# Two encoder layers with experts: low parts of split weights in place, two expert loads in the dense layer, the last unit in two loads

## The chip, the cores and the metric

The kernel runs on one core of a Trainium2 chip. A core has five engines that run side by side and meet only in semaphores: TensorE (PE), which multiplies matrices; VectorE (DVE); ScalarE (ACT); GpSimd (POOL); and SyncE (SP), which here only issues DMAs. Data come from HBM over 16 DMA engines into SBUF, 128 partitions wide; products gather in PSUM. The metric is the device time of one execution in microseconds. Before the change it is 1310.86 us, the median of three runs (1309.59 to 1312.39).

## The reference

Two layers over 256 tokens of width 1024, all float32. Each layer has a token mixer and a channel mixer, each between two norms. The channel mixer is a dense SwiGLU of width 4096 in layer 0; in layer 1 it is eight experts of width 3584, of which each token uses two.

```
for layer in range(2):
    proj = rmsnorm(h, mix_norm_pre[layer]) @ w_in[layer]            # 1024 -> 2048: u, q, k, v
    y_pool = pool_mixer(u, pool_w[layer], pool_scale[layer])         # windows of 2, 4, 8, 16 tokens
    y_na = neighbourhood_attention(q, k, v, na_rpb[layer])           # 16 heads of 32
    h = h + rmsnorm(concat(y_pool, y_na) @ w_out[layer], mix_norm_post[layer])
    hn = rmsnorm(h, ffn_norm_pre[layer])
    f = swiglu(hn, dense...) if layer == 0 else moe_swiglu(hn, router, gate, up, down)
    h = h + rmsnorm(f, ffn_norm_post[layer])
```

## The kernel before

**Split weights.** Outside the experts, PE works on float32 weights that are split in two: `w_hi`, a rounded copy that ACT makes (L1189), and `w_lo`, the rest, that DVE makes by subtraction (L1424, and L1435 for a piece of one). A product is three matmuls (L730 to L732: hi by hi, lo by hi, hi by lo). Weights arrive in 36 loads of 2 MB: 6 for the mixer of layer 0, 24 for the dense layer (gate, up, down in turns, eight blocks), 6 for the mixer of layer 1. They go round a ring of `RING` = 3 buffers (`ring`). Each load is worked in two halves, so there are 72 halves; `w_hi` and `w_lo` have `STAGE` = 3 buffers of half a load each. Three semaphores count halves: `hi_ready` (ACT's copy made), `split_ready` (DVE's rest made), `half_done` (PE's products made). Below, "half 40" is the first half of load 20.

**Who waits for what.** SP issues load n once `split_ready` says that both halves of load n-3 are split (L458), because then nobody reads the ring buffer any more. ACT copies half k when its load has landed and `half_done` has passed half k-3 (its `w_hi` buffer is free). DVE follows ACT, PE follows DVE.

**Experts.** Each expert's weights (gate, up, down) are 24 units of 3584 columns, 1.835 MB each, 192 in all, loaded by SP (L502) into 12 slots of SBUF (`SLOTS`), one after the other round the slots; unit n takes the slot of unit n-12 once PE has counted that one in `unit_done`. Most of the slots lie over memory that the mixer of layer 1 uses before them: bias table, `qT`, `kT`, `vv`, ring, `w_hi`, `w_lo`, `h`. So the first 12 units each wait for the last use of what lies below them. Slot 10 (`H_SLOT`) lies over `h` and `gpost`, which come back by two DMAs (L534, L535) once that slot is free for good; that is why `SLOT_OF` sends the last but one unit to slot 11.

**An expert on PE.** The tokens of an expert are gathered into 3 groups of 32 (in some of the eight turns, 2 groups; the order of turns is 3, 2, 3, 3, 2, 3, 3, 2). Gate and up take eight units each (L1077), down takes the last eight (L1086), two at a time: the first of a pair is used for three tiles of 1024 columns, then a fourth tile lies over both, then three tiles lie in the second. ACT applies silu (L1376), DVE multiplies and transposes (L1744, L1749), and ACT copies the result `y` out (L1382). Then PE spreads it back over the tokens (`combine`; for the last turn `combine_end`, L1047), DVE and ACT make the last norm, and SP stores the result. If an expert had more tokens than its turn holds, up to five extra turns would follow in a loop; with these inputs the loop runs through without work.

**ACT's tables.** ACT must load a table before it uses another family of functions. `last_norm` begins with such a load (L1265, for the square root), after the loop of extra turns.

## Time and profile before

| | |
|---|---|
| median of three runs | 1310.86 us (1309.59 to 1312.39) |
| span of the profiled execution | 1308.4 us |
| the profiled execution's own time | not given apart from its span; the three runs lie 1.2 to 4.0 us above the span, their median 2.5 us |
| PE busy | 1285.0 us, 98% |
| DVE, ACT, POOL busy | 409.0, 286.0, 108.4 us |
| weights and other data read from HBM | 439.36 MB |
| DMA queue of SP | 433.58 MB, 81.4% of the 16 engines' span |

The span runs from the first to the last instruction of the profiled execution; all positions below are microseconds from its start. The mixer of layer 0 fills about 10 to 98 us, the dense layer 110 to 375, the mixer of layer 1 382 to 470, norm and routing up to 489, the eight experts 489 to 1295, the last norm and the store the rest. A busy PE is not a PE at its peak: its matmuls are pipelined and their ends modelled. What counts is what it waits for.

### The profile page before, as it was taken

To read this page: it belongs to the slowest core of one execution; us is meant where nothing else is said; L and a number is where in the kernel's file an instruction comes from. 1 tells how busy PE (TensorE), PEld (TensorE's weight loads), DVE (VectorE), ACT (ScalarE), POOL (GpSimd) and SP (SyncE) were. 2 spreads that over 40 slices of the span, in tenths; PEclk is the share of its full clock that TensorE was granted. 3 is DMA by queue.
4 is the path that set the end of the run, shared out by engine and by line. 5 is a ranking of instruction groups with operands and counts; after the bars stand their busy time and mean duration, and the time that the engine had idled before them with its cause. 6 is when DMAs were issued, how large, how long until landed. Compare 5 with 4: busy or idle time off the path is not lost.

```text
span 1308.4 us, 31062 instructions
## 1 busy us (share of the span) xinstructions
PE 1285.0 (98%) x14397; PEld 794.5 (61%) x14397; DVE 409.0 (31%) x565; ACT 286.0 (22%) x433; POOL 108.4 (8%) x240
## 2 busy tenths in 40 slices
PE   9999999999999999999999999999999999999996
PEld 8888999999989863354353364345353355336443
DVE  6886555555567850030210120030030031021011
ACT  4666344444466630000000000000000000000101
POOL 3334200000000307300000000000000000000000
PEclk9999999999999989999999999999999999999999
DMA  9646855555543399999999999999999999999994
GB/s 303 221 175 211 259 193 193 193 193 193 193 158 141 146 425 427 425 421 398 427 424 426 426 424 425 425 425 425 425 424 425 425 426 424 425 426 424 426 425 187
DMA packets 67012, 443.50 MB, mean 339 GB/s; under 512 B 4520, under 2 KB 10800, under 8 KB 42304
## 3 DMA queue, kind: packets, MB, share of 16 engines
q1 hardware_dynamic: 64736, 433.58, 81.4%
q0 software_dynamic: 2144, 7.90, 2.1%
q8 instruction: 115, 1.88, 0.6%
q14 instruction: 17, 0.14, 0.0%
HBM read 439.36 MB, written 2.10 MB: 337 GB/s over the span
## 4 chain that ended last, share of the span: by engine, by line
PE 90%; DMA 4%; DVE 2%; ACT 1%; SPq 1%; issue 1%; ACTq 0%; DVEq 0%
PE psum L1077 38%; PE psum L1086 18%; PE psum L730 9%; PE psum L732 9%; PE psum L731 9%; DMA unit<-in_moe_w_down 3%; PE psum L1021 2%; PE psum L1032 1%; PE psum L827 1%; DMA ring<-in_w_in 1%; PE psum L818 1%; SPq L385 1%; PE psum L844 1%; ACT pt L1230 1%; PE psum L759 1%
## 5 line engine op out<-in xcount | busy, mean ns | idle before, releaser
L1077 PE MATMUL psum<-unit,xT 128*32 128x448 f32 x5376 | 507.0, 539 | 0.1
L1077 PEld LDWEIGHTS psum<-unit,xT 128*32 128x32 f32 x5376 | 174.9, 110 | 326.9 <-issue 324.8
L1086 PE MATMUL psum<-unit,hid 128*32 128x256 f32 x4704 | 259.1, 380 | 2.4 <-DMA unit<-in_moe_w_down 2.4
L1086 PEld LDWEIGHTS psum<-unit,hid 128*32 128x32 f32 x4704 | 152.0, 110 | 107.0 <-issue 5.3
L1744 DVE TENSOR_TENSOR hidp<-hid,psum 128x448 f32<-128x448 f32 x42 | 38.4, 915 | 535.4 <-PE psum L1077 535.4
L1424 DVE TENSOR_TENSOR w_lo<-ring,w_hi 128x2048 fp32r<-128x2048 f32 x64 | 149.9, 2350 | 112.8 <-ACT w_hi L1189 112.5
L730 PE MATMUL psum<-hT_hi,w_hi 128*128 128x256 f32 x656 | 183.3, 279 | 0.1
L732 PE MATMUL psum<-hT_hi,w_lo 128*128 128x256 f32 x656 | 182.1, 278 | 0.0
L731 PE MATMUL psum<-hT_lo,w_hi 128*128 128x256 f32 x656 | 182.1, 278 | 0.0
L1189 ACT ACTIVATE w_hi<-ring 128x2048 fp32r<-128x2048 f32 x71 | 135.1, 1910 | 59.2 <-PE psum L732 53.0
L730 PEld LDWEIGHTS psum<-hT_hi,w_hi 128*128 128x128 f32 x656 | 123.2, 188 | 2.0 <-issue 1.4
L731 PEld LDWEIGHTS psum<-hT_lo,w_hi 128*128 128x128 f32 x656 | 123.8, 189 | 0.3
L732 PEld LDWEIGHTS psum<-hT_hi,w_lo 128*128 128x128 f32 x656 | 123.2, 188 | 0.0
L1364 ACT ACTIVATE spread<-psum 128x768 f32<-128x768 f32 (+1 forms) x8 | 5.8, 730 | 399.0 <-PE psum L1064 399.0
L1376 ACT ACTIVATE hid<-psum 128x448 f32<-128x448 f32 x42 | 22.8, 543 | 221.2 <-PE psum L1077 220.8
L1724 DVE TENSOR_TENSOR facc<-facc,psum 128x512 f32<-128x512 f32 x28 | 17.4, 683 | 112.4 <-PE psum L1032 112.4
L732 PE MATMUL psum<-w_hi,dhid_lo 128*128 128x512 f32 x128 | 50.5, 395 | 0.0
L731 PE MATMUL psum<-w_lo,dhid_hi 128*128 128x512 f32 x128 | 50.3, 393 | 0.0
L730 PE MATMUL psum<-w_hi,dhid_hi 128*128 128x512 f32 x128 | 49.9, 390 | 0.0
L1382 ACT ACTIVATE y<-psum 128x512 f32<-128x512 f32 x8 | 4.8, 597 | 155.3 <-PE psum L1086 155.3
L1749 DVE STREAM_TRANSPOSE hid<-hidp 128x448 f32<-128x448 f32 x42 | 27.1, 645 | 1.9
L731 PEld LDWEIGHTS psum<-w_lo,dhid_hi 128*128 128x128 f32 x128 | 24.1, 188 | 5.3
(253 smaller groups left out, 947.9 us busy)
## 6 DMA issues: line engine op xcount, KB each, us to landing
unit<-in_moe_w_gate SPq DMA_DIRECT2D x64, 1792.0 KB, 31.8
unit<-in_moe_w_up SPq DMA_DIRECT2D x64, 1792.0 KB, 26.3
unit<-in_moe_w_down SPq DMA_DIRECT2D x64, 1792.0 KB, 31.2
ring<-in_dense_w_gate SPq DMA_DIRECT2D x8, 2048.0 KB, 9.1
ring<-in_dense_w_up SPq DMA_DIRECT2D x8, 2048.0 KB, 9.0
ring<-in_dense_w_down SPq DMA_DIRECT2D x8, 2048.0 KB, 8.2
ring<-in_w_in SPq DMA_DIRECT2D x6, 2048.0 KB, 8.7
ring<-in_w_out SPq DMA_DIRECT2D x4, 2048.0 KB, 8.8
```

Source lines behind the costliest of these rows:

```text
L730: mm(dst, still[0], moving[0], start=start, stop=False)
L731: mm(dst, still[0], moving[1], start=False, stop=False)
L732: return mm(dst, still[1], moving[0], start=False, stop=stop)
L1021: ins = mm(gather_out[s][quad(j)], pick[:, t, Q * s:Q * (s + 1)], blocks, start=t == 0, stop=t == NT - 1)
L1077: ins = mm(bank(half, s)[quad(j)], xT[:, s, dt, :], w[:, at:at + FJ], start=dt == 0, stop=dt == DT - 1)
L1086: ins = mm(down_out[s][quad(j)], e[:, half, s, t, :], w, start=half == t == 0 and s != 2, stop=half == 1 and t == FT - 1, skip_group_check ...
L1189: act.activation(hi, src, ACT.Copy).then_inc(hi_ready, 1)
L1376: act.activation(hid[:, half, s, :], bank(half, s), ACT.Silu).then_inc(silu_done, bank_step(s, groups))
L1424: dve.tensor_tensor(lo, src, hi.bitcast(F32), ALU.subtract).then_inc(split_ready, 1)
L1724: ins = dve.tensor_tensor(part, part, outs[j].rearrange("p (t n) -> p t n", t=NT), ALU.add)
L1744: dve.tensor_tensor(buf.rearrange("p t r -> p r t"), hid[:, half, s, :].rearrange("p (r t) -> p r t", t=FT), bank(half, s).rearrange("p (r ...
L1749: dve.transpose(hid[:, half, s, :], buf.rearrange("p t r -> p (t r)")).then_inc(e_ready, bank_step(s, groups))
```

## The change

- `w_lo` has no buffers of its own any more. DVE writes the low part over the half of the ring buffer that it was made from (`ring_lo`). A ring buffer is then free only when PE has used it, so SP's wait before load n is on `half_done` of load n-3 and no longer on `split_ready`.
- The 24 KB of each partition that this frees, and some more from moved small buffers (`win_b`, `win_c`, `win_d`, `prob_b`), hold `early`: two slots that nothing else uses. Units 0 and 1 are loaded into them in the dense layer, behind its loads 8 and 16 (counted from 0). The other ten slots lie over the mixer's memory in a new order, so the first waits of units 2 to 11 change.
- `H_SLOT` is 11. Only the last unit leaves the round of the slots: it goes to slot 0.
- The last unit (unit 191) comes in two loads: columns 0 to 2559, counted as before, and columns 2560 to 3583 under a semaphore of their own, `last_landed`. PE works two of the last three tiles for both groups of tokens, waits for `last_landed`, then works the last tile for both.
- ACT loads the square root's table after the last turn's silu instead of at the start of `last_norm`.
- In the norm after the mixer of layer 1, ACT's squares go to `junk` instead of `pt23`.

The core of the diff:

```diff
-assert 2 * MOE0 % STAGE == 0
+EARLY_UNITS = (8, 16)
-H_SLOT = 10
+H_SLOT = 11
+LAST_CUT = UNIT - D
-SLOT_OF = [n % SLOTS for n in range(N_UNITS - 2)] + [SLOTS - 1, 0]
+SLOT_OF = [n % SLOTS for n in range(N_UNITS - 1)] + [0]
...
+        ring_lo = [sb(f"ring_lo{k}", [P, 8 * C4], F32R, over=f"ring{k}") for k in range(RING)]
-        w_lo = sb("w_lo", [P, STAGE, 8 * C2], F32R)
...
                 if seq >= RING:
-                    sp.wait_ge(split_ready, 2 * (seq - RING) + 2)
+                    sp.wait_ge(half_done, 2 * (seq - RING) + 2)
...
+                if isinstance(i, int) and (i, u) == (NE - 1, UNITS - 1):
+                    sp.dma_start(units[slot][:, 0:LAST_CUT], src[:, 0:LAST_CUT]).then_inc(unit_landed[slot], 16)
+                    sp.dma_start(units[slot][:, LAST_CUT:UNIT], src[:, LAST_CUT:UNIT]).then_inc(last_landed, 16)
+                    return
...
+                if j in EARLY_UNITS:
+                    load_unit(0, zeroth, EARLY_UNITS.index(j))
+            load_mixing(1)
+            sp.wait_ge(half_done, MH - 4)
+            load_unit(0, zeroth, 2)
             sp.wait_ge(scored, GROUPS * DEPTH)
-            load_unit(0, zeroth, 0)
+            load_unit(0, zeroth, 3)
+            load_unit(0, zeroth, 4)
+            sp.wait_ge(pv_done, GROUPS * DEPTH)
+            sp.wait_ge(half_done, MH - 2)
+            load_unit(0, zeroth, 5)
+            sp.wait_ge(half_done, MH)
+            for u in range(6, 10):
+                load_unit(0, zeroth, u)
+            sp.wait_ge(delta_ready, 3 * DEPTH)
             sp.wait_ge(delta_dve_ready, DEPTH)
-            load_unit(0, zeroth, 1)
...
+            load_unit(0, zeroth, 10)
             sp.wait_ge(h_parked, 16 * NT)
             sp.wait_ge(hs_ready, 2 * 4)
-            load_unit(0, zeroth, 10)
             sp.wait_ge(logits_done, 1)
             load_unit(0, zeroth, 11)
...
+                    if last and v == DT - 2:
+                        for s in range(groups):
+                            project_hidden(half, h0, range(row + 4, row + 6), s)
+                        pe.wait_ge(last_landed, 16)
+                        for s in range(groups):
+                            ins = project_hidden(half, h0, range(row + 6, row + 7), s)
...
             def last_norm(value):
-                act.preload_act_table(ACT.Sqrt)
...
+                if last or extra:
+                    act.preload_act_table(ACT.Sqrt)
```

What this does to the order of instructions is seen at three places. First SP, before the experts: the last load of the mixer of layer 1 (`ring`) and the first units. The number behind `unit` names the slot: 112 to 123 are slots 0 to 11 in the kernel before, 118 to 129 in the changed one.

Before:

```order
L465 DMA ring<-in_w_out 128x4x1024 [waits split_ready] x2
L502 DMA unit_112<-in_moe_w_gate 128x3584 [waits scored]
L502 DMA unit_113<-in_moe_w_gate 128x3584 [waits delta_dve_ready]
L502 DMA unit_114<-in_moe_w_gate 128x3584 [waits split_ready,delta_ready,pv_done]
L502 DMA unit_115<-in_moe_w_gate 128x3584 [waits split_ready]
L502 DMA unit_116<-in_moe_w_gate 128x3584 [waits split_ready]
L502 DMA unit_117<-in_moe_w_gate 128x3584 [waits half_done]
L502 DMA unit_118<-in_moe_w_gate 128x3584 [waits half_done]
L502 DMA unit_119<-in_moe_w_gate 128x3584 [waits half_done]
L502 DMA unit_120<-in_moe_w_up 128x3584 [waits half_done]
L502 DMA unit_121<-in_moe_w_up 128x3584 [waits rms_post]
L502 DMA unit_122<-in_moe_w_up 128x3584 [waits hs_ready,h_parked]
```

Changed (units 0 and 1, slots 118 and 119, stand 23 and 14 rows further up, among the dense layer's loads):

```order
L467 DMA ring_56<-in_w_out 128x4x1024 [waits half_done]
L500 DMA unit_120<-in_moe_w_gate 128x3584 [waits half_done]
L500 DMA unit_121<-in_moe_w_gate 128x3584 [waits scored]
L500 DMA unit_122<-in_moe_w_gate 128x3584
L500 DMA unit_123<-in_moe_w_gate 128x3584 [waits half_done,pv_done]
L500 DMA unit_124<-in_moe_w_gate 128x3584 [waits half_done]
L500 DMA unit_125<-in_moe_w_gate 128x3584
L500 DMA unit_126<-in_moe_w_up 128x3584
L500 DMA unit_127<-in_moe_w_up 128x3584
L500 DMA unit_128<-in_moe_w_up 128x3584 [waits delta_dve_ready,delta_ready]
L500 DMA unit_129<-in_moe_w_up 128x3584 [waits logits_done,hs_ready,h_parked]
```

Ten units are left to issue here where there were twelve. Unit 2 waits for half 67 of the mixer now, unit 5 for half 69, and units 6 to 9 for the last one, half 71.

Second PE, at the end of the last expert: `unit_123` before and `unit_128` now hold unit 190, `unit_112` and `unit_118` hold unit 191, and `hid` is the hidden layer.

Before:

```order
L1086 MATMUL psum<-unit_123,hid 32x256 [waits unit_landed11]
L1086 MATMUL psum<-unit_123,hid 32x256 x23
L1086 MATMUL psum<-unit_123,hid 32x256 [waits unit_landed0]
L1086 MATMUL psum<-unit_123,hid 32x256
L1086 MATMUL psum<-unit_112,hid 32x256 x2
L1086 MATMUL psum<-unit_123,hid 32x256 x2
L1086 MATMUL psum<-unit_112,hid 32x256 x26
L1047 MATMUL psum<-y,spread 128x256 [waits spread_ready,y_act]
```

Changed:

```order
L1092 MATMUL psum<-unit_128,hid 32x256 [waits unit_landed10]
L1092 MATMUL psum<-unit_128,hid 32x256 x23
L1092 MATMUL psum<-unit_128,hid 32x256 [waits unit_landed0]
L1092 MATMUL psum<-unit_128,hid 32x256
L1092 MATMUL psum<-unit_118,hid 32x256 x2
L1092 MATMUL psum<-unit_128,hid 32x256 x2
L1092 MATMUL psum<-unit_118,hid 32x256 x18
L1092 MATMUL psum<-unit_118,hid 32x256 [waits last_landed]
L1092 MATMUL psum<-unit_118,hid 32x256 x7
L1053 MATMUL psum<-y,spread 128x256 [waits spread_ready,y_act]
```

Of the 28 matmuls that read the last unit, 20 now need only its first load, and 8 stand behind a wait for the second.

Third ACT, from the last expert's silu (`hid`) to the last norm; two rows of the loop of extra turns stand between the groups of the first piece.

Before, the silu, the copy of `y` and the start of the loop, and then the start of `last_norm`:

```order
L1376 ACTIVATE hid<-psum 128x448 [waits gate_done] x3
L1376 ACTIVATE hid<-psum 128x448 [waits unit_done]
L1382 ACTIVATE y<-psum 128x512 [waits unit_done]
L1402 TENSOR_LOAD plan [waits plan_ready]
L1402 ISA x2
L1265 ACT_TABLE_LOAD
L1267 ISA
L1199 ACTIVATE pt_58,st<-psum 128x1024 [waits gained,comb_done]
```

Changed, from the same silu:

```order
L1390 ACTIVATE hid<-psum 128x448 [waits gate_done] x3
L1390 ACTIVATE hid<-psum 128x448 [waits unit_done]
L1393 ACT_TABLE_LOAD
L1398 ACTIVATE y<-psum 128x512 [waits unit_done]
L1418 TENSOR_LOAD plan [waits plan_ready]
L1418 ISA x2
```

The table load stands ahead of the copy of `y` instead of behind the loop.

## Rows read from the trace of the kernel before

**Rows 1.** The page: what the DMA engines moved, in 40 slices of 32.7 us.
```profile
GB/s 303 221 175 211 259 193 193 193 193 193 193 158 141 146 425 427 425 421 398 427 424 426 426 424 425 425 425 425 425 424 425 425 426 424 425 426 424 426 425 187
```

**Rows 2.** Chain that ended last, in order: start, us, what.
```profile
1255.93 35.30 DMA unit<-in_moe_w_down
...
1291.27 3.70 PE psum L1086 x64
...
1296.86 1.24 DVE hs L1536
```

**Rows 3.** PE's waits: us in total, times, longest.
```profile
PE psum L1086 <- DMA unit<-in_moe_w_down: 2.4, 3, 1.1
```

**Rows 4.** Timeline of PE, end of the last expert: start, us, what, [idle before].
```profile
1274.22 3.66 PE L1086 MATMUL psum<-unit,hid 128*32 128x256 f32 x64 [0.78 <-DMA unit<-in_moe_w_down]
1278.45 2.80 PE L1086 MATMUL psum<-unit,hid 128*32 128x256 f32 x48 [0.56 <-DMA unit<-in_moe_w_down]
...
1283.96 6.25 PE L1086 MATMUL psum<-unit,hid 128*32 128x256 f32 x112
1291.27 3.66 PE L1086 MATMUL psum<-unit,hid 128*32 128x256 f32 x64 [1.06 <-DMA unit<-in_moe_w_down]
```

**Rows 5.** DMAs issued from 1255.5 to 1257 us: KB each, us to landing.
```profile
unit<-in_moe_w_down SPq DMA_DIRECT2D x1, 1792.0 KB, 35.3
...
gpost<-in_ffn_norm_post SPq DMA_DIRECT2D x1, 512.0 KB, 38.2
```

**Rows 6.** Timeline of SP: the last issue on that queue before the store.
```profile
1256.79 7.17 SPq L535 DMA_DIRECT2D gpost<-in_ffn_norm_post  x1
```

**Rows 7.** Timelines of ACT and DVE, the last norm.
```profile
1297.94 1.28 ACT L1265 ACT_TABLE_LOAD   x1 [2.34 <-issue]
1299.23 1.02 ACT L1199 ACTIVATE pt<-psum 128x1024 f32<-128x1024 f32 x1
...
1299.00 1.22 DVE L1536 TENSOR_TENSOR hs<-psum,gpost 128x1024 f32<-128x1024 f32 x1 [0.91 <-PE psum L1047]
1300.77 0.16 DVE L1442 RECIPROCAL st<-st 128x1 f32<-128x1 f32 x1 [0.55 <-ACT st L1193]
```

**Rows 8.** Unit loads with their latency: one issued at 596.59 us, then one at 603.48.
```profile
unit<-in_moe_w_up SPq DMA_DIRECT2D x1, 1792.0 KB, 7.5
...
unit<-in_moe_w_up SPq DMA_DIRECT2D x1, 1792.0 KB, 10.3
```

**Rows 9.** Stretches: length, busy PE, PEld, DVE, ACT, POOL, PEclk, DMA share, GB/s.
```profile
590.00:600.00 10.00, 10.00 (x192) 5.96 (x184) 0.00 (x0) 0.00 (x0) 0.00 (x0) 1.00 0.96 365
600.00:1212.00 612.00, 612.00 (x8220) 273.51 (x8216) 79.50 (x151) 26.50 (x48) 0.00 (x0) 1.00 1.01 425
```

**Rows 10.** Dense layer, load 20: SP's issue; ACT at half ends; DVE's split and product.
```profile
232.84 0.37 SPq L465 DMA_DIRECT2D ring<-in_dense_w_gate  x1
...
243.65 0.60 ACT L1352 ACTIVATE dsilu<-psum 128x512 f32<-128x512 f32 x1 [3.03 <-PE psum L732]
254.69 1.92 ACT L1189 ACTIVATE w_hi<-ring 128x2048 fp32r<-128x2048 f32 x1 [3.64 <-PE psum L732]
...
256.65 2.29 DVE L1424 TENSOR_TENSOR w_lo<-ring,w_hi 128x2048 fp32r<-128x2048 f32 x1 [3.26 <-ACT w_hi L1189]
265.54 0.69 DVE L1628 TENSOR_TENSOR dsilu<-dsilu,psum 128x512 f32<-128x512 f32 x1
```

**Rows 11.** Ring loads with their latency, issued at 232.84, at 116.40 and at 121.61 us.
```profile
ring<-in_dense_w_gate SPq DMA_DIRECT2D x1, 2048.0 KB, 9.1
...
ring<-in_dense_w_down SPq DMA_DIRECT2D x1, 2048.0 KB, 12.0
...
ring<-in_dense_w_up SPq DMA_DIRECT2D x1, 2048.0 KB, 20.9
```

**Rows 12.** Timeline of ACT: PE ends half 13, and half 17.
```profile
122.51 0.60 ACT L1352 ACTIVATE dsilu<-psum 128x512 f32<-128x512 f32 x1 [3.25 <-PE psum L732]
...
145.12 0.60 ACT L1352 ACTIVATE dsilu<-psum 128x512 f32<-128x512 f32 x1 [3.25 <-PE psum L732]
```

More of the change, by code:

```diff
@@ L132, in hybrid_encoder @@
         addr = {}
+        early = sb("early", [P, len(EARLY_UNITS) * UNIT])
+        ring = [sb("ring0", [P, 8 * C4])]
         bias = sb("bias", [P, HEADS * 2 * ROWS * WIN])
@@ L136, in hybrid_encoder @@
         vv = sb("vv", [P, NT, C4])
+        ring += [sb(f"ring{k}", [P, 8 * C4]) for k in range(1, RING)]
+        ring_lo = [sb(f"ring_lo{k}", [P, 8 * C4], F32R, over=f"ring{k}") for k in range(RING)]
+        w_hi = sb("w_hi", [P, STAGE, 8 * C2], F32R)
+        prob_b = sb("prob_b", [P, 2, 4, ROWS, COLS])
+        uT = sb("uT", [P, 4, S + 2 * POOL_PAD])
         win_a = sb("win_a", [P, S + 2 * POOL_PAD])
-        ring = sb("ring", [P, RING, 8 * C4])
-        w_hi = sb("w_hi", [P, STAGE, 8 * C2], F32R)
-        w_lo = sb("w_lo", [P, STAGE, 8 * C2], F32R)
-        uT = sb("uT", [P, 4, S + 2 * POOL_PAD])
         pt23 = sb("pt23", [P, 2, D])
+        sb("gap", [P, (addr["early"] + 4 * UNIT * H_SLOT - plan_top[0]) // 4])
         h = sb("h", [P, NT, D])
         gpost = sb("gpost", [P, D])
-        win_b = sb("win_b", [P, S + 2 * POOL_PAD])
         router_sb = sb("router_sb", [P, DT, Q])
@@ L148, in hybrid_encoder @@
         cols = sb("cols", [P, 8])
-        assert addr["bias"] + 4 * UNIT * H_SLOT <= addr["h"] and addr["win_b"] <= addr["bias"] + 4 * UNIT * (H_SLOT + 1)
-        sb("spare", [P, (addr["bias"] + 4 * UNIT * SLOTS - plan_top[0]) // 4])
+        sb("spare", [P, (addr["early"] + 4 * UNIT * SLOTS - plan_top[0]) // 4])
         hs = sb("hs", [P, NT, D])
@@ L200, in hybrid_encoder @@
         spread = sb("spread", [P, NT, TG, P], over="gpre")
-        units = [sb(f"unit{k}", [P, UNIT], over="bias", skip=4 * UNIT * k) for k in range(SLOTS)]
+        units = [sb(f"unit{k}", [P, UNIT], over="early", skip=4 * UNIT * k) for k in range(SLOTS)]
         ident = cst[:, K_ID:K_ID + P]
@@ L475, in by_tile, with load_mixing @@
                 return w.rearrange("(t p) n -> p t n", p=P)
-            for layer in range(DEPTH):
+            def load_mixing(layer):
                 s0 = mixing_first_load(layer)
@@ L483, in _ @@
                 load(s0 + 5, wo[:, 0:4, :], 4)
-                if layer == 0:
-                    for j, (what, b) in enumerate(DENSE):
-                        cut = slice(b * C4, (b + 1) * C4)
-                        if what == "down":
-                            load(MIX_LOADS + j, by_tile(d_down[0, cut]), 4)
-                        else:
-                            w = d_gate if what == "gate" else d_up
-                            load(MIX_LOADS + j, by_tile(w[0])[:, :, cut], DT)
             def load_unit(i, expert, u):
@@ L736, in split_half @@
                 pe.wait_ge(split_ready, n + 1)
-                return w_hi[:, n % STAGE, :], w_lo[:, n % STAGE, :]
+                return halves(n)[1:]
             def open_half(n, dsts, half):
-                w = [a.rearrange("p (t n) -> p t n", t=DT) for a in (w_hi[:, half % STAGE, :], w_lo[:, half % STAGE, :])]
+                w = halves(half)[1:]
                 pe.wait_ge(hT_hi_ready, 4 * n + 4)
@@ L1146, in expert_item @@
                         gather(i + 1, after)
-                    for s in range(groups):
-                        ins = project_hidden(half, h0, range(row + 4, row + 7), s)
+                    if last and v == DT - 2:
[4 more added lines that the diff above has]
+                            ins = project_hidden(half, h0, range(row + 6, row + 7), s)
+                    else:
+                        for s in range(groups):
+                            ins = project_hidden(half, h0, range(row + 4, row + 7), s)
                     ins.then_inc(unit_done, 1)
@@ L1427, in split_part @@
             def split_part(k, part):
-                src, hi, lo = halves(k // 2, rows_first(k // 2))[k % 2]
-                if rows_first(k // 2):
-                    cut = (slice(None), slice(part * 4 * C2, (part + 1) * 4 * C2))
-                else:
-                    cut = (slice(None), slice(part * 4, (part + 1) * 4))
+                src, hi, lo = halves(k)
+                tiles = src.shape[1] // 2
+                cut = (slice(None), slice(part * tiles, (part + 1) * tiles))
                 dve.wait_ge(hi_ready, k + 1)
```

71 lines of the change are left out of this document (33 added, 38 removed).

## Prediction

> **What bounds the kernel now.** I read the slices of the page first. From slice 15 to the last but one (458 us to the end of the experts) the DMA engines move about 425 GB/s [rows 1]. That looks like a kernel bound by its loads, and 8.6 us of loads moved elsewhere (two units of 1.835 MB at 425 GB/s, 4.3 us each) look like 8.6 us won. The stretches say otherwise: from 600 to 1212 us PE is busy for 612.00 of 612.00 us while the DMA engines move 425 GB/s [rows 9]. Both are full; the turns with 3 groups give PE more to do than a turn's loads cost, those with 2 groups less. What decides is who waits for whom, so I read PE's waits next: over the whole span PE waits for units 3 times, 2.4 us in all [rows 3]. The timeline shows the three at the very end, 0.78, 0.56 and 1.06 us [rows 4]. The chain of waits has the last unit's DMA in it for 35.3 us [rows 2], but that is 35.3 us in a queue beside a busy PE; it ends at 1291.23, and PE could have gone on at 1290.21 (1283.96 + 6.25) [rows 4]. So earlier loads can give 2.4 us to PE and no more. Behind the last matmul the norm is a chain between DVE and ACT [rows 2, 7].
>
> **How far the lead of two units carries.** Units 0 and 1 are in SBUF long before 489 us, so the queue is ahead at the start. But there are still 12 slots, and in the first turn, with 3 groups, PE frees them slower than the queue fills them. Before the change the queue had already caught up with PE: the unit issued at 596.59 landed 7.5 us later, where 4.3 us are pure transfer and nothing stood in front of it, and in 590 to 600 us only 365 GB/s moved [rows 8, 9]. A queue that is further ahead just runs dry sooner there: the unit issued at 596.59 cannot be issued before PE frees its slot. What survives is what the dry spell cost afterwards. The unit issued at 603.48 landed at 613.8 (10.3 us later) [rows 8]; counted from 604.1 with two transfers of 4.3 us it could land at 612.7, so 1.1 us; by the rate it is (425 - 365) x 10 us = 0.6 MB, 1.4 us [rows 9]. Bounds 0 and 1.4 us. I take 0.5, since part of the gap may be a hiccup that comes anyway. From there to the end the queue never runs dry [rows 9], so all later units land 0.5 us earlier.
>
> **The last unit in two loads.** The last four tiles are 32 matmuls in 3.66 us, 0.114 us each [rows 4], and all waited for the whole unit. Now 24 of them wait for the first 2560 of 3584 columns, which land 4.3 x 1024/3584 = 1.2 us before the rest, at 1290.0 without any lead. PE is ready at 1290.21, so the third wait goes (1.06 us). The 24 matmuls take to 1292.95; the rest landed at 1291.2, so the last 8 follow without a wait and end at 1293.9. PE gains 1.06 us, and on top the lead, since the first two waits shrink by it one for one: 1.06 + 0.5 = 1.56 us. Below, the gain is 0 if the halves of the unit don't land one after the other; above, all three waits go, 2.4 us.
>
> What is late next: `gpost` must be back before DVE's first product. It was issued at 1256.79 and landed 38.2 us later, at 1295.0; DVE started at 1296.86 [rows 2, 5, 6]. Slack 1.9 us; with PE 1.56 us earlier and the queue 0.5 us earlier, 0.8 us are left. It holds.
>
> The Trainium skill ("DMA: Bandwidth & Descriptors", section on the anatomy of one DMA) has a fixed cost of about 2 us for each DMA, whatever its size. By that rule alone a second load for the last 1024 columns would land at 1293.2, 0.3 us after PE wants it, and the split would give 0.8 us, not 1.06. The trace speaks against adding it within a full queue: at 425 GB/s a unit takes 4.3 us, with no 2 us between units [rows 9].
>
> **The table load.** ACT's load ran from 1297.94 to 1299.22, and the first square started behind it, at 1299.23; its input had been ready since 1298.10 (1296.86 + 1.24) [rows 2, 7]. Moved behind the last silu it lies in ACT's wait for PE's down product, and costs nothing. The square gains 1.1 us, but DVE is busy with its second product until 1300.22 and then idles only 0.55 us for ACT [rows 7]. So the end gains at most 0.55 us. ACT's second square needs that second product, which lets it start 0.3 us earlier than before and its root end 0.4 us before the old time. I take 0.4; bounds 0 and 0.55.
>
> **Ring loads that wait for PE.** Take load 20 of the dense layer. It was issued at 232.84, when half 35 was split. Now it waits until PE has used half 35, at 243.65, 10.8 us later [rows 10]. It lands 9.1 us after issue [rows 11], at 252.8. ACT can't copy it before 254.69 anyway, since it waits for PE there (its `w_hi` buffer) [rows 10]. So nothing moves, with 1.9 us to spare. ACT's copy (1.92), DVE's split (to 258.94) and PE's end of the half before (265.54) leave 6.6 us more [rows 10]: PE stalls only if a load is 8.5 us late. An early unit in front costs 4.3 us: hidden. In the mixers PE takes longer per half, so there is more room. The wait queues nothing but loads behind it on SP.
>
> The tight place is 116 to 150 us, where the bias words share the engines: latencies of 12.0 and 20.9 us [rows 11]. Load 9 (halves 18 and 19) will be issued at 122.51, when PE ends half 13, and PE wants half 18 at 145.12 [rows 12]; less 1.9 and 2.3 us for copy and split, it may take 18.4 us. The 20.9 us of the load issued at 121.61 include waiting for the one in front, which landed at 128.4; alone it took 14.1 us. Now nothing is in front. It holds with 4.3 us to spare; bounds 0 and 5.1 us (below). The low part written in place is the same DVE instruction over the same columns, read with the same stride and written with it: 0, as nothing in the rows prices a stride; if it cost 0.5 us each, the 6.6 us would still cover it. One more DMA issue, `junk` for `pt23` and the moved small buffers: 0 for each, off PE's path.
>
> The routing before 489 us waits for no unit, so the experts start when they did.
>
> **The sum.** 1308.4 - 1.06 - 0.5 - 0.4 = 1306.4 us of span. The median of the runs lies 2.5 us above the profiled span: 1308.9 us, 2.0 us or 0.15% faster. A measurement of this kernel can tell about 0.2%, 2.6 us, from no change.
>
> **Rivals.**
> 1. *The lead reaches the end.* If the gap near 600 us was wholly a dry spell and the slots give more than I think, all of PE's 2.4 us go, and the table's 0.4: 2.8 us, 1308.1. For it: a full queue in every slice [rows 1]. Against: the 7.5 us at 596.59 [rows 8]. It can't be more, whatever the loads do: PE is the bound from 489 us on.
> 2. *Nothing reaches the end.* The last unit's two loads end together, or `h` and `gpost` are late behind them and DVE starts where it did: 0 to 0.5 us, 1310.6. For it: only 0.8 us of slack at `gpost`.
> 3. *Slower: ring loads come too late in the contended stretch.* If load 9 again takes 20.9 us, it passes 18.4 by 2.5, PE stalls that long, and load 10, issued just as late, does it again: 5.1 us lost, 2.0 won, 1314.0. It decides from a latency of 18.4 us. For it: DMA rates there are split with the bias words. Against: in-order service, 14.1 us.
> 4. *The change does not do what it says:* if the early units are not in place, or slots are freed later in the new order, PE waits near 489 us. Unit 0 is wanted at 489 us and unit 11 some 45 us after, so there is room; I see no price, and count it in rival 2.
>
> **How the numbers follow.** Forecast 0.55, rival 1 0.2, rivals 2 and 4 0.12, rival 3 0.13. Runs of one kernel spread over 2.8 us, so 2.0 us can come out as 2.7: a fifth of the forecast and over half of rival 1 fall beyond 0.2% faster, 0.11 + 0.13, and some for gains that I have not seen: 0.28. Slower by over 0.2%: most of rival 3, 0.11. Within 0.2%: 0.61. The range, 1306.8 to 1312.2, takes in both ends of the terms (0 to 2.95 us) with the spread and leaves most of rival 3 and a little below out.
>
> **What would show it.** Right: no PE wait for a unit but two below 0.8 us near 1274 and 1278; none before the last tile; a DMA rate clearly under 425 GB/s before 600 us, lower than before; no table load behind the experts; the experts starting at 489; dense halves ending where they did. Wrong: PE waiting for DVE's low parts between 130 and 160 us, the last unit landing over 1.5 us earlier, or DVE's first product waiting for `gpost`.

## Result and the profile after

The changed kernel takes 1319.26 us (median of 4 runs, 1316.69 to 1319.85); the kernel before took 1310.22 us (median of 4 runs, 1307.53 to 1312.39). The ratio is 1.0066, 95% interval 1.0045 to 1.0086: 0.7% slower, where 0.15% faster was predicted. It is outside the range of the prediction too. The profiled execution of after took 1316.69 us with a span of 1314.8 us, 6.4 us more than the span of before.

The page after, the DMA slices (32.9 us each) that answer to [rows 1]:

```profile
GB/s 302 219 118 228 231 242 181 181 234 179 185 231 129 147 314 427 426 420 387 428 424 425 426 425 425 426 426 423 426 425 424 427 425 424 425 426 425 424 426 207
```

Units 0 and 1, issued at 180.2 and 270.5 us, lie in the slices of 242 and 234; the slice at 592 to 625 us (387) holds the dry spell. The chain of waits after, start and length, answers to [rows 2]; its first row is the first product of the experts:

```profile
496.77 72.37 PE psum L1083 x768
...
1251.41 35.15 DMA unit<-in_moe_w_down
1286.61 2.80 PE psum L1092 x48
1289.40 2.79 PE psum L1062 x12
1292.19 9.79 PE psum L1092 x176
1302.66 1.15 PE psum L1053 x16
```

In the trace before, the same view has

```profile
489.12 72.37 PE psum L1077 x768
```

So the experts start 7.65 us later. From there to the end of the span it was 819.3 us (1308.4 - 489.12) and is 818.0 us now: about 1.25 us less. All of the loss lies ahead of the experts; 7.65 - 1.25 = 6.4 us.

PE's waits for units, and the timeline of PE at the end, answer to [rows 3, 4]:

```profile
PE psum L1092 <- DMA unit<-in_moe_w_down: 1.9, 2, 1.2
```

```profile
1282.30 3.66 PE L1092 MATMUL psum<-unit,hid 128*32 128x256 f32 x64 [1.22 <-DMA unit<-in_moe_w_down]
1286.61 2.80 PE L1092 MATMUL psum<-unit,hid 128*32 128x256 f32 x48 [0.64 <-DMA unit<-in_moe_w_down]
...
1292.12 9.82 PE L1092 MATMUL psum<-unit,hid 128*32 128x256 f32 x176
```

The third wait, for the last unit, is gone: 176 matmuls now stand in one row where [rows 4] has 112 and 64 with 1.06 us between them. The first two waits grew from 1.34 to 1.86 us together. The two parts of the last unit landed at 1298.24 and 1299.48 us.

The stretches (same columns as [rows 9]), and the unit issued at 604.2 us, 7.6 us after its fellow of [rows 8]:

```profile
590.00:600.00 10.00, 10.00 (x182) 5.96 (x178) 0.78 (x2) 0.81 (x1) 0.00 (x0) 1.00 0.94 370
600.00:1212.00 612.00, 612.00 (x8220) 272.56 (x8216) 79.55 (x151) 26.53 (x48) 0.00 (x0) 1.00 1.01 424
598.00:608.00 10.00, 10.00 (x192) 6.01 (x188) 0.00 (x0) 0.00 (x0) 0.00 (x0) 1.00 0.96 352
```

```profile
unit<-in_moe_w_up SPq DMA_DIRECT2D x1, 1792.0 KB, 9.4
```

The last norm, timelines of ACT and DVE, answers to [rows 7]; no table load stands there any more, and DVE's wait for ACT is 0.25 us instead of 0.55. From PE's last product of the last expert to the start of DVE's last product it is 7.12 us where it was 7.43:

```profile
1305.20 1.02 ACT L1212 ACTIVATE pt<-psum 128x1024 f32<-128x1024 f32 x1 [2.59 <-DVE hs L1550]
```

```profile
1306.01 1.22 DVE L1550 TENSOR_TENSOR hs<-psum,gpost 128x1024 f32<-128x1024 f32 x1 [0.91 <-PE psum L1053]
...
1308.87 0.16 DVE L1456 RECIPROCAL st<-st 128x1 f32<-128x1 f32 x1 [0.25 <-ACT st L1206]
```

**Where the 7.65 us are.** The page's groups, busy time, mean of one, and idle time before (last column), first before, then after:

```profile
L730 PE MATMUL psum<-hT_hi,w_hi 128*128 128x256 f32 x656 | 183.3, 279 | 0.1
L732 PE MATMUL psum<-hT_hi,w_lo 128*128 128x256 f32 x656 | 182.1, 278 | 0.0
L731 PE MATMUL psum<-hT_lo,w_hi 128*128 128x256 f32 x656 | 182.1, 278 | 0.0
```

```profile
L738 PE MATMUL psum<-hT_hi,w_hi 128*128 128x256 f32 x656 | 186.6, 285 | 0.0
L739 PE MATMUL psum<-hT_lo,w_hi 128*128 128x256 f32 x656 | 185.6, 283 | 0.0
L740 PE MATMUL psum<-hT_hi,ring_lo 128*128 128x256 f32 x656 | 185.6, 283 | 0.0
```

The last column says that PE does not wait in these groups, before or after. The mean of one rose by 5 to 6 ns. Since matmuls overlap, the mean is a latency, and what counts is the distance from start to start. It is read from ACT, which copies `psum` when PE ends a half of gate or up. Two such copies, one half apart, before and after:

```profile
205.43 0.60 ACT L1352 ACTIVATE dsilu<-psum 128x512 f32<-128x512 f32 x1 [2.28 <-PE psum L732]
210.88 0.60 ACT L1352 ACTIVATE dsilu<-psum 128x512 f32<-128x512 f32 x1 [3.04 <-PE psum L732]
```

```profile
207.96 0.60 ACT L1364 ACTIVATE dsilu<-psum 128x512 f32<-128x512 f32 x1 [2.60 <-PE psum L740]
213.72 0.60 ACT L1364 ACTIVATE dsilu<-psum 128x512 f32<-128x512 f32 x1 [3.36 <-PE psum L740]
```

A half has 48 such matmuls (8 blocks of the contraction, 2 of the columns, 3 products). Before: 5.45 us here and 5.44 to 5.45 in the others of this level, 113.3 ns each. After: 5.76 us, 120.0 ns. In the stretch of [rows 12] it was already slower before: (145.12 - 122.51) / 4 = 5.65 us, 117.8 ns. The medians of the distance from start to start in the whole trace say the same: in the kernel before 26 of the gate and up halves 13 to 57 run at 113.3 ns and 5 at 117.8, as do halves 61 and 62 of the second mixer; after, all 33 run at 120.0. That is 26 x 0.32 + 5 x 0.11 = 8.9 us for the dense layer and 0.2 for the two of the second mixer; the 512-column products of down give back 0.8 (a mean distance of 227.3 ns for 228.9 to 233.4). The traces agree: the first of these products in the second mixer starts 8.0 us later than before (390.3 for 382.3), the last group of them 9.0 us later (449.1 for 440.1). From there to the experts it takes 47.7 us where it took 49.0, which is no gain of the change, since a second profile of the kernel before (e13) has 47.7 too.

PE is granted its full clock in both traces and is busy all the time. A stretch of 100 us in the dense layer, before and after (columns as in [rows 9]), has PEclk 1.00 in both, but 728 matmuls before and 714 after:

```profile
150.00:250.00 100.00, 100.00 (x728) 93.76 (x728) 49.41 (x30) 41.45 (x31) 0.00 (x0) 1.00 0.54 196
150.00:250.00 100.00, 100.00 (x714) 94.64 (x713) 47.83 (x30) 40.44 (x30) 0.00 (x0) 1.00 0.55 201
```

PE's matmuls here are the same in number and shape. What else differs for these matmuls is where their operands lie. The change moved `win_a`, 1088 bytes, from ahead of the ring to behind `uT`. Worked out from the buffers' sizes, the start of the operands, counted from the first buffer, modulo 2048 bytes per partition:

```
                         ring   w_hi   low part   hT_hi, hT_lo
before                   1088   1088   1088       0
after                       0      0   0          0
```

### The profile page after: what moved, and what is told of

Its sections match the earlier page's. It is cut to its first block, busy times and chain, and to the rows that moved or that the text cites. A ratio compares the mean times of both kernels' runs of the same rounds, so it can differ in the third digit from the quotient of the medians.

```text
span 1314.8 us, 31066 instructions
## 1 busy us (share of the span) xinstructions
PE 1294.0 (98%) x14397; PEld 803.8 (61%) x14397; DVE 406.8 (31%) x565; ACT 286.2 (22%) x433; POOL 109.0 (8%) x240
## 4 chain that ended last, share of the span: by engine, by line
PE 90%; DMA 4%; DVE 2%; ACT 1%; SPq 1%; issue 0%; ACTq 0%; DVEq 0%
PE psum L1083 37%; PE psum L1092 19%; PE psum L738 9%; PE psum L739 9%; PE psum L740 9%; DMA unit<-in_moe_w_down 3%; PE psum L1027 1%; PE psum L1038 1%; PE psum L835 1%; DMA ring<-in_w_in 1%; PE psum L826 1%; SPq L387 1%; PE psum L852 1%; PE psum L767 1%; ACT pt L1243 1%; DVE hs L1539 0%
## 5 line engine op out<-in xcount | busy, mean ns | idle before, releaser
L738 PE MATMUL psum<-hT_hi,w_hi 128*128 128x256 f32 x656 | 186.6, 285 | 0.0
L739 PE MATMUL psum<-hT_lo,w_hi 128*128 128x256 f32 x656 | 185.6, 283 | 0.0
L740 PE MATMUL psum<-hT_hi,ring_lo 128*128 128x256 f32 x656 | 185.6, 283 | 0.0
L1440 DVE TENSOR_TENSOR ring_lo<-ring,w_hi 128x2048 fp32r<-128x2048 f32 x64 | 148.6, 2330 | 118.3 <-ACT w_hi L1202 118.0
L738 PEld LDWEIGHTS psum<-hT_hi,w_hi 128*128 128x128 f32 x656 | 125.8, 192 | 1.9 <-issue 1.4
L739 PEld LDWEIGHTS psum<-hT_lo,w_hi 128*128 128x128 f32 x656 | 125.8, 192 | 0.3
L740 PEld LDWEIGHTS psum<-hT_hi,ring_lo 128*128 128x128 f32 x656 | 125.8, 192 | 0.0
L738 PE MATMUL psum<-w_hi,dhid_hi 128*128 128x512 f32 x128 | 49.9, 390 | 0.0
L739 PE MATMUL psum<-ring_lo,dhid_hi 128*128 128x512 f32 x128 | 49.9, 390 | 0.0
L740 PE MATMUL psum<-w_hi,dhid_lo 128*128 128x512 f32 x128 | 49.8, 389 | 0.0
L740 PEld LDWEIGHTS psum<-w_hi,dhid_lo 128*128 128x128 f32 x128 | 24.0, 188 | 5.0
```

Source lines behind the costliest of these rows:

```text
L738: mm(dst, still[0], moving[0], start=start, stop=False)
L739: mm(dst, still[0], moving[1], start=False, stop=False)
L740: return mm(dst, still[1], moving[0], start=False, stop=stop)
L1440: dve.tensor_tensor(lo, src, hi.bitcast(F32), ALU.subtract).then_inc(split_ready, 1)
```

## Experiments

Theory: the place of the weight blocks relative to the tokens' parts sets the distance of the 256-column matmuls, and that is the whole loss. Rivals: the low part written in place (DVE and DMA touch the buffers that PE reads), or the early units and the new order of the loads. The unit of offset below is bytes per partition. Each ratio is to runs of the kernel before on the same chip, and several chips were used, so across experiments the ratios compare better than the medians.

**e1, the kernel before with `win_a` moved behind `w_lo`, nothing else.**

```diff
-        win_a = sb("win_a", [P, S + 2 * POOL_PAD])
         ring = sb("ring", [P, RING, 8 * C4])
         w_hi = sb("w_hi", [P, STAGE, 8 * C2], F32R)
         w_lo = sb("w_lo", [P, STAGE, 8 * C2], F32R)
+        win_a = sb("win_a", [P, S + 2 * POOL_PAD])
```

> The kernel before with one buffer moved: win_a (1088 bytes a partition) stands behind w_lo instead of ahead of the ring, so ring, w_hi and w_lo begin at multiples of 2048 bytes from the first buffer (32768, 81920, 106496) instead of 1088 beyond one (33856, 83008, 107584). Nothing else changes. Theory P (placement: PE's 256-column matmuls go at 120.0 ns instead of 113.3 because the weights lie at the same offset as the tokens hT): a dense half of gate or up takes 5.76 us instead of 5.44, the experts start 7 to 8 us later, the time is 7 to 9 us over before. Rival S (the low part in the ring, with a stride of two halves): 113.3 ns as before, time as before within 2 us. Rival I (something that goes with the program as a whole, such as its instruction stream): as before too, since the streams are the same.

Measured: 1321.06 us, ratio 1.0093 (1.0073 to 1.0113). It has the instructions of before, with PE's matmuls in the same order. ACT's two copies and the start of the experts:

```profile
208.29 0.60 ACT L1352 ACTIVATE dsilu<-psum 128x512 f32<-128x512 f32 x1 [2.61 <-PE psum L732]
214.05 0.60 ACT L1352 ACTIVATE dsilu<-psum 128x512 f32<-128x512 f32 x1 [3.36 <-PE psum L732]
```

```profile
498.42 72.36 PE psum L1077 x768
```

5.76 us a half, 120.0 ns, and experts 9.3 us later than in the first trace of before, a little more than the 7 to 8 expected. One buffer of 1088 bytes that moves makes the kernel before as slow as the changed one, without any other edit. This is the cause, shown from one side.

**e2 and e3, the kernel after with 64 or 512 bytes ahead of the ring; e6, e7, e8 the same with 32, 128 and 256.**

```diff
         early = sb("early", [P, len(EARLY_UNITS) * UNIT])
+        sb("pad", [P, 16])
         ring = [sb("ring0", [P, 8 * C4])]
```

> The changed kernel with 64 unused bytes a partition ahead of the first ring buffer, so that ring, ring_lo and w_hi begin 64 bytes beyond a multiple of 2048; taken from the unused gap, nothing else changes. Theory P with an offset within 128 bytes as its cause: 113.3 ns a matmul, halves of 5.44 us, time 8 to 10 us under the changed kernel, about 1308 to 1310. Theory P with a larger unit (banks of memory): no change, 1317 to 1320. Rivals S and I: 1317 to 1320.

> As the run with 64 bytes, with 512. Theory P with an offset within 128 bytes as its cause: no change from the changed kernel, 1317 to 1320, as 512 keeps the offset within 128. Theory P with a unit of 1024 bytes or more: 113.3 ns, 1308 to 1310. Rivals S and I: 1317 to 1320.

> The changed kernel with 32 unused bytes ahead of the first ring buffer. If the offset counts in units of 32 bytes or less: as with 64 bytes, halves under 5.7 us. If in units of 64: 5.76 us, as without padding.

> The changed kernel with 128 unused bytes ahead of the first ring buffer. If the pattern repeats every 128 bytes: 5.76 us a half, as without padding. If it repeats every 256 or 512 bytes: 5.44 to 5.65 us.

> The changed kernel with 256 unused bytes ahead of the first ring buffer. If the pattern repeats every 128 or 256 bytes: 5.76 us a half. If it repeats only every 512: 5.44 to 5.65 us.

Measured (e6 to e8 are single runs, so they have no ratio; length of a half in the dense layer, from ACT's copies near 207 and 213 us):

```
offset      half, us   experts start   time, us   ratio to before
0 (after)   5.76       496.77          1319.26    1.0066
32 (e6)     5.68       494.85          1314.8
64 (e2)     5.65       493.50          1313.37    1.0023 (1.0011 to 1.0036)
128 (e7)    5.76       496.29          1316.61
256 (e8)    5.76       498.16          1319.66
512 (e3)    5.76       497.04          1318.90    1.0075 (1.0056 to 1.0095)
```

A pad of 64 bytes, with no other edit, gives back 5.9 us of 9.0, not all of it as expected: its dense halves run at 117.8 ns and not at 113.3. 512 and 256 give nothing back. It is the offset and not the order of the buffers, and it is not "any offset helps". The modulus of 2048 is no more than a way to write the offsets down: 0, 128, 256 and 512 leave no remainder when divided by 128 and have halves of 5.76 us; 64 and the 1088 of before both leave 64 and have 5.44 to 5.66; 32 lies between. So every row fits a pattern that repeats every 128 bytes, as the expectation of e7 has it. Other offsets were not run.

**e4, the kernel before with the last unit in two loads and the table load moved.**

```diff
+                if isinstance(i, int) and (i, u) == (NE - 1, UNITS - 1):
+                    sp.dma_start(units[slot][:, 0:UNIT - D], src[:, 0:UNIT - D]).then_inc(unit_landed[slot], 16)
+                    sp.dma_start(units[slot][:, UNIT - D:UNIT], src[:, UNIT - D:UNIT]).then_inc(last_landed, 16)
+                    return
...
-                act.preload_act_table(ACT.Sqrt)
...
+                if last or extra:
+                    act.preload_act_table(ACT.Sqrt)
```

> The kernel before with the two edits at its end alone: the last unit in two loads with the wait for the second ahead of the last tile, and the square root's table loaded behind the last silu. Prediction's terms: 1.06 us for the split and 0.4 for the table, 1.5 us of span between the last unit's landing and the end: 15.7 instead of 17.2 us; in the time, 1.5 us under before. Rival (the second load lands 2 us behind the first, and DVE waits for gpost): 0 to 0.8 us.

Measured: 1307.78 us, ratio 0.9979 (0.9964 to 0.9994), 0.8 to 4.7 us faster than before, and the only kernel here whose interval lies below 1. PE at its end:

```profile
1273.18 3.66 PE L1091 MATMUL psum<-unit,hid 128*32 128x256 f32 x64 [0.92 <-DMA unit<-in_moe_w_down]
1277.49 2.80 PE L1091 MATMUL psum<-unit,hid 128*32 128x256 f32 x48 [0.65 <-DMA unit<-in_moe_w_down]
...
1283.01 9.74 PE L1091 MATMUL psum<-unit,hid 128*32 128x256 f32 x176
```

From the first matmul of the experts (487.94) to the end of this row (1292.75) it takes 804.8 us; before, 805.8 (489.12 to 1294.93). From there to the end of the span 12.8 us, before 13.5.

The second part splits in two. From the end of PE's row to the start of DVE's last product it takes 7.13 us, 7.43 before: 0.3 us, and this is the table load's share. It is the same in every trace here: 7.43 in the four without the moved table load (before, e13, e1, e5), 7.12 or 7.13 in the twelve with it. The other 0.33 us lie behind that product (5.70 for 6.03), where the change does nothing; the kernel before has 5.75 there in its second profile and e1 6.37.

The 1.0 us of the two loads is less firm than it looks. The third wait, 1.03 to 1.06 us in the four traces with one load, is gone here, in after and in seven of the other ten traces with two; in e6 and e12 PE waits 0.27 and 0.18 us for the first part. The second part lands 1.24 to 1.26 us behind the first. But in e10 PE waits 1.37 us for the first part, and the waits ahead of it move by more than 1.06 us from one profile to the next: the kernel before needs 805.8 us of PE in one profile and 807.2 in the other, the kernels with two loads 804.8 to 807.4.

**e5, the kernel before with the low part in place and ring loads that wait for PE, every buffer at its old offset** (the room of `w_lo` stays empty).

```diff
-        w_lo = sb("w_lo", [P, STAGE, 8 * C2], F32R)
+        sb("w_lo_room", [P, STAGE, 8 * C2])
+        ring_lo = [sb(f"ring_lo{k}", [P, 8 * C4], F32R, over="ring", skip=32 * C4 * k) for k in range(RING)]
...
-                    sp.wait_ge(split_ready, 2 * (seq - RING) + 2)
+                    sp.wait_ge(half_done, 2 * (seq - RING) + 2)
...
-                sp.wait_ge(split_ready, 2 * (MOE0 - 4 + u))
+                sp.wait_ge(half_done, 2 * (MOE0 - 4 + u))
```

> The kernel before with the low parts written over the ring and the ring loads waiting for PE, as in the change, but with every buffer where it was: the room of w_lo stays empty, ring and w_hi keep their offset of 1088 bytes. Units 2 to 4 wait for PE's halves too (unit 4 for the last one). Theory P (placement): halves of 5.44 to 5.65 us as before, experts start within 1 us of before, time within 3 us of before. Rival S (the stride or the place of the low part costs too): halves of gate and up stay over 5.6 us all through the dense layer, time 3 to 5 us over before, which would be the rest that 64 bytes of padding left.

Measured: 1316.21 us, ratio 1.0064 (1.0047 to 1.0081), as slow as after, but for another reason. Chain, PE's waits and stretches:

```profile
485.35 72.37 PE psum L1079 x768
```

```profile
PE psum L1088 <- DMA unit<-in_moe_w_down: 9.0, 8, 1.6
```

```profile
590.00:600.00 10.00, 10.00 (x164) 5.16 (x160) 0.00 (x0) 0.87 (x2) 0.00 (x0) 1.00 1.02 432
600.00:1212.00 612.00, 608.23 (x8168) 269.91 (x8160) 79.55 (x151) 25.62 (x46) 0.00 (x0) 1.00 1.01 425
```

The in-place write costs PE nothing: gate and up halves of 5.44 us throughout, and the experts start 3.8 us earlier than in the first trace of before, 1.5 us earlier than in its second (e13). But units 2 to 4 wait for PE's halves now, and go out at 448.0, 456.8 and 467.8 us where before it was 450.4, 452.7 and 459.5; unit 5 lands at 480.7, before at 475.3. The slack of [rows 8, 9] is gone: at 590 to 600 us the DMA engines move 432 GB/s where it was 365, and PE, which was busy for 612.00 of 612.00 us, has 608.23. The dry spell is gone, and from unit 5 on each unit lands 2.4 to 5.4 us later than before, up to the last (1295.3 for 1291.2). From the experts' first product to PE's last it takes 813.7 us for 805.8, and PE waits 9.0 us for units instead of 2.4. So PE and the queue bound this kernel almost equally: when PE reaches the experts 3.8 us earlier and the loads start 5.4 us later, the queue sets the end. Both expectations failed: the halves are fast, but the time is not that of before. In the changed kernel unit 5 lands at 476.4 us with the experts starting at 496.77, so it does not get there. That is not due to the early units alone: e10 below has none of them, and its unit 5 lands at 476.0.

**e9, the kernel after with `win_a` ahead of the ring again** (offset 1088; unit 2 also waits for the last use of `win_a`) **and e14, the same once more; e10, the same with units 0 and 1 loaded behind the second mixer's loads instead of early.**

```diff
         early = sb("early", [P, len(EARLY_UNITS) * UNIT])
+        win_a = sb("win_a", [P, S + 2 * POOL_PAD])
         ring = [sb("ring0", [P, 8 * C4])]
...
-        win_a = sb("win_a", [P, S + 2 * POOL_PAD])
...
             sp.wait_ge(half_done, MH - 4)
+            sp.wait_ge(delta_ready, 3 * DEPTH)
             load_unit(0, zeroth, 2)
```

> The kernel after with one buffer moved and one wait added: `win_a` (1088 bytes) stands again ahead of the ring, so ring, `w_hi` and the buffers behind them start 1088 bytes off the multiples of 2048 at which the tokens' parts lie, as in the kernel before; unit 2 also waits for the last use of `win_a`, whose place its slot now covers. Early units, low parts in the ring, the two loads of the last unit and the moved table load stay. Theory (placement is what cost the time): the 256-column matmuls of the dense layer run at 113 ns, or 113 to 118, start to start and not at 120; a half of gate or up takes 5.44 to 5.65 us; the experts start at 485 to 489 us of the span and not at 496.8; from there 800.5 us of PE to the end of the first unit's successors and the shorter tail, a span of 1303.4 to 1307, a time of 1305 to 1309, ratio to before 0.996 to 0.999. Rival 1 (the low parts in the ring cost the time by accesses that collide, wherever the ring lies): 120 ns, experts from 496, a time of 1317 to 1320. Rival 2 (the placement matters, but with the faster dense layer the unit loads end the span, as in the run with low parts in the ring and no early units, whose experts took 827 us): experts start at 485 and PE waits for units 5 to 9 us, a time of 1310 to 1315.

> The kernel with `win_a` put back, unchanged, profiled again. Fixed by the program: 117.8 ns in halves 20 to 57 again, 113.3 in 13 to 17 and 61 to 62, experts start at 490.7. Varies with the execution: another pattern, experts start 485 to 494.

> The same kernel without the two early unit loads: units 0 and 1 are loaded behind the ring loads of the second layer. It prices the early loads when the matmuls are fast. Theory (the experts' stage is bound by the queue once PE reaches it earlier, and two units already loaded give 8 to 9 us of queue back): experts start at the same time as with the early loads within 0.5 us, units land 4 to 9 us later, PE waits for units at the end 4 to 9 us instead of 2, a time 3 to 6 us above that of the kernel with early loads. Rival (the lead is used up whatever it was, as the step in the prediction had it): within 1 us of the kernel with early loads.

Measured: e9 1311.74 us, ratio 1.0007 (0.9994 to 1.002): the loss is gone, and no gain is left; 1305 to 1309 us had been expected. ACT's copies in e9:

```profile
205.31 0.60 ACT L1365 ACTIVATE dsilu<-psum 128x512 f32<-128x512 f32 x1 [2.49 <-PE psum L741]
210.97 0.60 ACT L1365 ACTIVATE dsilu<-psum 128x512 f32<-128x512 f32 x1 [3.25 <-PE psum L741]
```

5.66 us, 117.8 ns, in the dense layer where the kernel before has 113.3; in halves 13 to 17 it is the other way round, 113.3 for 117.8. The experts start at 490.71 us and not at 485 to 489. That is where the gain went: 1.6 us later than in the first trace of before up to the experts, 1.5 us shorter from there. e14 (1311.41 us, one run) has 117.8 in the dense layer again, but 117.8 also in halves 13 to 17, and starts the experts at 491.45. e10: 1312.66 us, ratio 1.0019 (1.0004 to 1.0034); PE waits 3.9 us for units instead of 1.7 (2.3 in e14), and the medians differ by 0.9 us with intervals that overlap. The 3 to 6 us that I had expected of the early units are not there; the rival (within 1 us) is what came.

**e11, the kernel after with `win_a` directly ahead of `w_hi`:** the ring stays at 0, `w_hi` goes to 1088.

> The kernel after with `win_a` moved directly ahead of `w_hi`: the ring's three buffers stay at multiples of 2048 bytes, `w_hi` (and what stands behind it) lies 1088 bytes off. It tells whose place matters. If PE's interval goes by where its own moving operand lies: the product lines with the high part of the weight run at 113 to 118 ns, the one with the low part (read from the ring) stays at 120; a half takes 5.5 to 5.65 us. If by where the ring lies (DMA, ACT and VectorE write and read it) : 120 ns in all three, a half 5.76 us, experts from 496 to 497. If `w_hi` alone decides (ACT writes it while PE reads it): 113 to 118 in all three.

Measured: 1318.84 us in one run, experts at 498.44. The page's groups:

```profile
L739 PE MATMUL psum<-hT_lo,w_hi 128*128 128x256 f32 x656 | 186.8, 285 | 0.0
...
L738 PE MATMUL psum<-hT_hi,w_hi 128*128 128x256 f32 x656 | 186.0, 284 | 0.0
L740 PE MATMUL psum<-hT_hi,ring_lo 128*128 128x256 f32 x656 | 185.0, 282 | 0.0
```

All three expectations fail. The line that reads the ring, which lies at the slow place, is the fastest, and the line ahead of it is the slowest: from 156 us on, four halves run at 5.87 us, the next four at 5.65, and so on by turns. In those of 5.87 the distances after L738, L739 and L740 are 122, 127 and 118 ns, in those of 5.65 all three are 118. In the trace the weight loads lie beside the matmuls (94.64 us of weight loads in 100.00 us of a busy PE in the stretch above), so a block is loaded while the matmul ahead of it streams its tokens. The slow pair may be "tokens of L739 with the block for L740"; this fits the slow halves, but it is argued, not shown. The fast ones it does not explain: they use the same buffers at the same places, so what alternates is open.

**e12, the kernel after with the tokens' parts moved by 64 bytes instead of the weights.**

```diff
+        negmax = sb("negmax", [P, 2, 4])
+        sums = sb("sums", [P, 2, 4])
         hT_hi = sb("hT_hi", [P, DT, S], F32R)
```

> The kernel after with two small buffers (`negmax`, `sums`, 64 bytes together) moved ahead of `hT_hi`: the tokens' high and low parts lie 64 bytes off the multiples of 2048, ring and `w_hi` stay on them. If the distance between the two operands' places decides, as when the weights were moved by 64 bytes: 256-column matmuls at 113 to 118 ns, halves of 5.44 to 5.65 us, experts start at 492 to 494 us, a time of 1312 to 1315. If the weights' own place decides: 120.0 ns, 5.76 us, 496 to 497 us, 1317 to 1320.

Measured: 1315.05 us, ratio 1.0048 (1.0032 to 1.0065), experts at 494.40:

```profile
206.76 0.60 ACT L1364 ACTIVATE dsilu<-psum 128x512 f32<-128x512 f32 x1 [2.50 <-PE psum L740]
212.42 0.60 ACT L1364 ACTIVATE dsilu<-psum 128x512 f32<-128x512 f32 x1 [3.25 <-PE psum L740]
```

5.66 us, as in e2 (5.65). The weights lie where they lie in after; the tokens' parts moved, and with them the buffers behind them up to `delta`, which these products do not read. So in these products it is the relative place of the two operands that counts. The halves and the start of the experts show it; the ratio alone would not, since its interval touches that of after (1.0045 to 1.0086).

**e13, the kernel before, profiled once more.**

> The kernel before, unchanged, profiled again. If the level (113.3 or 117.8 ns) is fixed by the program, its halves 1 to 3 and 20 to 57 show 113.3 and 4, 5, 13 to 17 and 61 to 62 show 117.8 as in the first trace, experts start at 489.1. If it varies with the execution, other halves show 117.8 (or 113.3), and the experts start anywhere from 485 to 494.

```profile
486.80 72.37 PE psum L1077 x768
```

The run took 1309.15 us. Its halves 20 to 57 run at 113.3 ns and 13 to 17 at 117.8, as in the first trace, but 61 and 62 run at 113.3 for 117.8, and the experts start 2.3 us earlier. PE waits 3.6 us for units instead of 2.4. Some of the pattern stays with the program, and some changes from one execution to the next.

## Why the prediction was wrong

The step that failed is one clause: "One more DMA issue, `junk` for `pt23` and the moved small buffers: 0 for each, off PE's path". The small buffer `win_a` is off PE's path, but it stood ahead of the buffers that are on it. Taking it away shifted the ring and `w_hi` by 1088 bytes, onto the same offset modulo 2048 as the tokens' parts, and the 256-column matmuls went from 113.3 (at places 117.8) to 120.0 ns. That is 9.0 us up to the end of the second mixer in the profile, and 7.65 up to the experts. By itself it costs the kernel before 0.9% (e1), and with the place put back (e9) the changed kernel is at 1.0007, not at the predicted 0.9985: at the same offset of 1088 its dense layer runs at 117.8 ns where the kernel before has 113.3, some 5.5 us over 26 halves, and why is open. No bound of mine covered it, since I gave moved buffers a cost only through who waits for them. The sentence "the experts start when they did" fell with it, and two of the signs named for a right prediction, the experts starting at 489 and the dense halves ending where they did. The duration of a matmul was taken as given.

The other terms, in its order:

- *The last unit in two loads, 1.06 us.* The mechanism is right: the third wait is gone in e4 and in after. The size, 1.0 us in e4, is within the scatter of the waits ahead. The estimate by the Trainium skill ("DMA: Bandwidth & Descriptors", section on the anatomy of one DMA), whose figure of about 2 us is a fit for loads issued by GpSimd and not, as here, by SP, would have left a wait of 0.3 us before the last 8 matmuls; none is in the rows, and the second part landed 1.24 us behind the first, which at 425 GB/s is its transfer alone.
- *The table load, 0.4, bounds 0 and 0.55.* Right: 0.3 us, from 7.43 to 7.12 us up to DVE's last product, in every trace.
- *The lead of the early units, 0.5, bounds 0 and 1.4.* The mechanism is right: the queue is dry again around 600 us, 352 GB/s for 365 before. Nothing of the lead arrives at the end of after: the two waits that were to shrink by 0.5 us grew by 0.5. PE's waits scatter by 1.2 us between two profiles of before, so no more can be said than that it is small; e10, with units 0 and 1 loaded later, is slower by 0.9 us with intervals that overlap. But e5 shows what I had missed: the slack near 600 us is the margin by which PE, not the queue, bounds the kernel. "PE is the bound from 489 us on" holds only while the loads start in time.
- *`gpost`*: DVE's first product started 1303.87, behind PE and not behind a load. Right.
- *Ring loads and low parts in place, 0 on PE.* Right: the products' lines have 0.0 us of idle time, and e5 has the earliest start of the experts, 485.35.
- *Rivals.* 3, the only one on the slower side, gave 1314.0 by late ring loads; it did not happen. 1, 2 and 4 were not what happened.

The sum without the failed step points the right way, but its size is not confirmed by the profiles. From the experts' start to the end, after takes about 1.25 us less than the first trace of before, and e4 1.6 (817.7 for 819.3), where 1.96 was predicted; 0.33 us of either lie behind DVE's last product and are scatter, and the second profile of before needs 820.4 us for the same stretch. The runs of e4 say 0.8 to 4.7 us.

## What to carry to other kernels

When a change moves any buffer, write down the offsets of the two operands of the busiest matmuls before and after, and compare the difference with the table above. A difference of 0, 128, 256 or 512 bytes cost 6% per matmul here (120.0 for 113.3 ns), and 64 bytes of padding got about two thirds of the time back. It is something to measure, not a rule: the 512-column products here were faster at equal offsets, and one offset gave two levels. When PE is never idle and the time still rises, compare the distance from start to start in the same loop before looking at waits. And if a kernel gets faster ahead of a stage that has both its engine and its loads full, check that the loads start earlier by as much.

## What the hardware did that I had not expected

- 256-column float32r matmuls, all at the full granted clock with no idle time between them, run at three distances: 120.0 ns with operands 0, 256 or 512 bytes apart modulo 2048; 113.3 or 117.8 ns at 64 and at 1088 bytes; at 32 about 118.3, at 128 119 to 120. The Trainium skill ("TensorE: Matmul & The Clock Gate", section on the back-to-back issue gap) gives N/2.4 GHz + 2.5 ns for a matmul by itself and names no place in memory; for 256 columns an estimate by that formula is 109.2 ns. None of the levels here is that. The Trainium skill ("SBUF — State Buffer", section on SBUF's two separate sides) says that PE's port never waits on anyone. e1 shows that PE's rate can change with addresses alone, at the same instructions; whether it is PE's own two readings that meet, as e12 suggests, or something else, no run here shows.
- The 512-column products of down go the other way by less: a mean distance of 228.9 to 233.4 ns before, with operands 1088 bytes apart, and 227.3 in after and e1, with both at the same offset.
- Not settled: what picks 113.3 or 117.8 at one placement. The dense layer's halves 20 to 57 had the same level in both profiles of before (113.3) and in e9, e14 and e10 (117.8), all with the weights at 1088, and other halves changed between executions.
